# Which engine makes the low halves of the weight units between the third branch's projection and the output projection

## The reference

```python
def hybrid_layer(x, ...):
    h = rms_norm(x, norm1_g)
    z = h @ w_in
    ya, yb, yc, yd = retention(..), conformer_conv(..), spatial_gating(..), swa_attention(..)
    ys = jnp.stack([ya, yb, yc, yd], axis=2)
    branches = jnp.einsum('bsnc,ncd->bsnd', ys, w_branch)   # four projections, 512 -> 1024
    mix = jnp.sum(sigmoid(zg) * branches, axis=2)
    x = x + (mix @ w_out)                                   # 1024 -> 1024
    h = rms_norm(x, norm2_g)
    gt, up = jnp.split(h @ w_ffn_in, 2, axis=-1)
    return x + ((silu(gt) * up) @ w_ffn_out)
```

## Time and profile before

| | |
|---|---|
| median of 3 runs | 2315.18 us (2309.21 to 2315.8) |
| profiled execution, its own time | 2315.32 us |
| its span | 2313.9 us |
| TensorE's granted clock, mean | 0.988 of full speed |
| PE busy | 2202.0 us (95%) |
| PEld busy | 2047.3 us (88%) |
| DVE busy | 1401.4 us (61%) |
| ACT busy | 1195.0 us (52%) |
| POOL busy | 869.1 us (38%) |
| transfers | 369.58 MB, mean 160 GB/s |

### The profile page before, as it was taken

The page is one execution under the profiler, slowest core; times in us unless marked ns, Lnnn a source line. Parts: engine busy times, 40 slices in busy tenths (PEclk is TensorE's granted clock), DMA queues, the critical chain, the costliest instruction groups (busy, mean ns, idle before and its releaser), DMA issues.

```text
span 2313.9 us, 38008 instructions
## 1 busy us (share of the span) xinstructions
PE 2202.0 (95%) x15186; PEld 2047.3 (88%) x15186; DVE 1401.4 (61%) x2409; ACT 1195.0 (52%) x2050; POOL 869.1 (38%) x477
## 2 busy tenths in 40 slices
PE   8888889999999979999999999999999999899999
PEld 7888879999999867888888799898998889899997
DVE  5758761586844597666665764446664665546664
ACT  6546434554444696554555355555444355555443
POOL 5555366687600392000003666460000766461000
PEclk9999999999999999999999999999999999999999
DMA  6443355555565404666665545355565554345555
GB/s 224 137 123 108 118 158 170 173 165 177 178 184 183 136 1 127 191 194 194 194 192 183 173 146 159 109 159 166 183 184 176 155 155 158 115 148 166 182 184 161
DMA packets 102930, 369.58 MB, mean 160 GB/s; under 512 B 11362, under 2 KB 13794, under 8 KB 102116
## 3 DMA queue, kind: packets, MB, share of 16 engines
q1 hardware_dynamic: 102756, 367.15, 51.4%
HBM read 364.49 MB, written 2.62 MB: 159 GB/s over the span
## 4 chain that ended last, share of the span: by engine, by line
PE 74%; DVE 17%; ACT 6%; issue 2%; DMA 1%; POOL 1%; SPq 0%; DVEq 0%; ACTq 0%
PE stream_bank L530 13%; PE stream_bank L531 13%; PE stream_bank L532 13%; PE side_bank L530 10%; PE side_bank L532 10%; PE side_bank L531 10%; DVE first_hot L1961 2%; DVE experts L1951 2%; ACT unit_hi L1046 1%; PE side_bank L592 1%; DVE unit_lo L1556 1%; POOL unit_lo L2284 1%; ACT squares L1072 1%; PE side_bank L611 1%; DVE hot L1919 1%
## 5 line engine op out<-in xcount | busy, mean ns | idle before, releaser
L2284 POOL TENSOR_TENSOR unit_lo<-raw,unit_hi 128x1024 fp32r<-128x1024 f32 (+1 forms) x305 | 744.6, 2447 | 445.1 <-ACT unit_hi L1046 444.6
L1046 ACT ACTIVATE unit_hi<-raw 128x1024 fp32r<-128x1024 f32 (+1 forms) x678 | 708.0, 1045 | 188.3 <-PE side_bank L532 92.9
L1556 DVE TENSOR_TENSOR unit_lo<-raw,unit_hi 128x1024 fp32r<-128x1024 f32 x373 | 459.4, 1232 | 403.4 <-ACT unit_hi L1046 403.0
L530 PE MATMUL stream_bank<-hT_hi,unit_hi 128*128 128x256 f32 x1672 | 494.0, 295 | 3.5 <-DVE unit_lo L1556 3.5
L531 PE MATMUL stream_bank<-hT_lo,unit_hi 128*128 128x256 f32 x1672 | 477.8, 286 | 0.0
L532 PE MATMUL stream_bank<-hT_hi,unit_lo 128*128 128x256 f32 x1672 | 477.6, 286 | 0.0
L530 PEld LDWEIGHTS stream_bank<-hT_hi,unit_hi 128*128 128x128 f32 x1672 | 325.7, 195 | 12.3 <-issue 6.3
L530 PE MATMUL stream_bank<-h2T_hi,unit_hi 128*128 128x256 f32 x1152 | 327.4, 284 | 2.6 <-DVE unit_lo L1556 2.5
L531 PEld LDWEIGHTS stream_bank<-hT_lo,unit_hi 128*128 128x128 f32 x1672 | 325.8, 195 | 1.6
L531 PE MATMUL stream_bank<-h2T_lo,unit_hi 128*128 128x256 f32 x1152 | 326.7, 284 | 0.0
L532 PE MATMUL stream_bank<-h2T_hi,unit_lo 128*128 128x256 f32 x1152 | 326.6, 284 | 0.0
(11 more groups left out here) (341 smaller groups left out, 4099.2 us busy)
## 6 DMA issues: line engine op xcount, KB each, us to landing
raw<-in_peer_u_dram SPq DMA_DIRECT2D x128, 512.0 KB, 3.6
raw<-in_peer_v_dram SPq DMA_DIRECT2D x128, 512.0 KB, 4.2
raw<-in_gate_dram SPq DMA_DIRECT2D x64, 512.0 KB, 3.6
raw<-in_gt_dram SPq DMA_DIRECT2D x44, 512.0 KB, 3.6
raw<-in_up_dram SPq DMA_DIRECT2D x44, 512.0 KB, 3.7
raw<-in_ffn_out_dram SPq DMA_DIRECT2D x44, 512.0 KB, 4.0
raw<-in_branch_dram SPq DMA_DIRECT2D x32, 512.0 KB, 3.7
raw<-in_w_gate_dram SPq DMA_DIRECT2D x24, 512.0 KB, 3.6
```

Source lines behind the costliest of these rows:

```text
L530: mm(out, l.hi, r.hi, start=start, stop=False)
L1046: activation(k.unit_hi[n % SPLIT_SLOTS][:, 0:w], k.raw[n % RAW_SLOTS][:, 0:w], ACT.Copy).then_inc(k.sem("unit_hi"), 1)
L1556: V.tensor_tensor(k.unit_lo[s][:, 0:w], k.raw[n % RAW_SLOTS][:, 0:w], k.unit_hi[s][:, 0:w], ALU.subtract).then_inc(unit_lo, 1)
L2284: G.tensor_tensor(k.unit_lo[s][:, 0:w], k.raw[n % RAW_SLOTS][:, 0:w], k.unit_hi[s][:, 0:w], ALU.subtract).then_inc(k.sem("unit_lo_pool"), 1)
```

## The change

One bound of a range in `lo_count` is moved, once for each of the two hybrid layers. The range in which DVE makes every low half began eight units before the first feed-forward unit (the first `w_out` unit), plus AHEAD, so at unit 19. Now it begins at the first unit of the third branch projection, plus AHEAD, so at unit 11. Unit 12 divides by 8 and is DVE's already. So seven units for each layer (11 and 13 to 18), fourteen in all, go from POOL to DVE. Nothing else is changed: TensorE's, ACT's and SP's instructions keep their order, and wait for the same units' low halves on the other engine's semaphore.

```diff
@@ -265,7 +265,7 @@
 
         U = self.place_of
         alone = [(U["peer_u", LATE // 1024] + AHEAD, U["cg.0", 0] + AHEAD)]
-        alone += [(U[f"gt.{l}", 0] - 8 + AHEAD, U[f"ffn_out.{l}", KF - 1] + 1 + AHEAD) for l in range(LAYERS)]
+        alone += [(U[f"branch.{l}", BRANCH_ORDER[2] * KD // 2] + AHEAD, U[f"ffn_out.{l}", KF - 1] + 1 + AHEAD) for l in range(LAYERS)]
         self.lo_engine, self.lo_ready = [], []
         counts = {"dve": 0, "pool": 0}
         for n in range(len(self.plan)):
```

## The result

The median went from 2314.61 us (2309.21 to 2318.37, 14 runs) to 2319.53 us (2317.83 to 2323.31, 14 runs). The ratio is 1.0023, with a 95% interval of 1.0016 to 1.0031: slower by 3.7 to 7.2 us, 4.9 by the medians. That is within the 0.3% that I called "the same", and yet not nothing. The profiled execution took 2318.88 us, of which the span is the first line here.

What follows compares the result with a forecast made beforehand. TensorE was taken to bound the kernel, never waiting for POOL. Two layers at 1.6 us, 3.2 us in all, on a profiled 2315.32 us or a median of 2315.18 us gave 2318.4 us, range 2311 to 2325.

Steps and rivals of the forecast that it cites:

- Third projection, cost nothing: Low halves 11, 13, 14: each 1.23 us fits DVE's idle 1.46 us per unit, so no cost and no gain.
- The loop of 4.23 us: Fourth projection: DVE and ACT wait on each other, so each unit takes 4.23 us against TensorE's 2.88.
- Low half 19 late, PE idle 0.6 us: At `w_out`: low half 19 ends 0.5 us too late for TensorE, which idles 0.6 us.
- High half 22, low half 23, high half 26: Behind low half 19, loads and adds slip; high half 26 waits for its load until 1583.24, not 1581.62.
- 1.6 us a layer, 3.2 in both: Late high half 26 delays the second norm by 1.6 us per hybrid layer, containing PE's 0.6 us; bounds +1.0 and +3.8.
- The ports: DVE's splits no longer share SBUF ports with POOL: two holdups, 0.7 us a layer, freed without shortening the sum.
- The clock behind the turns stays at 1.00: After the second norm's turns in the hybrid layers, TensorE's granted clock was to stay 1.00, adding no cost.
- Rival 2: Long landings delay the norm and TensorE's clock falls behind the turns: 5.9 us a layer, 2327 us; chance 0.14.
- hide part of the 1.9 us: First hybrid layer: a longer wait could hide part of the 1.9 us of issue behind the turns; given no value.

Runs made afterwards that it cites:

- e1: Kernel before with only the third projection's low halves (11, 13, 14) moved to DVE; 2315.19 us, ratio 1.0004 to before.
- e4: Changed kernel, but in the fourth projection DVE makes the low half between the sum and its split, not ahead of the product; 2313.63 us, ratio 0.9996 to before.
- e5: Changed kernel with unit 26's high half moved behind the norm's squares on ACT, its low half behind the diagonal on DVE; 2314.57 us, ratio 1.0005 to before.
- e2: Kernel before with only the fourth projection's low halves (15 to 18) moved to DVE; 2319.13 us, ratio 1.0019 to before.
- e3: Changed kernel with 10 instead of 8 spare matmuls ahead of the second norm's turns in each hybrid layer; 2318.57 us, ratio 1.0015 to before.
- e9: Changed kernel with the hybrid layers' spare matmuls replaced by 21 on split operands with 512 columns; 2318.96 us, ratio 1.0024 to before.
- e7: Kernel before with two useless ACT copies ahead of the second norm's squares in each hybrid layer, no low half moved; 2318.91 us, ratio 1.0019 to before.
- e11: Kernel before with 11 instead of 8 spare matmuls ahead of the second norm's turns in the hybrid layers; 2316.26 us, ratio 1.0016 to before.
- e8: Changed kernel measured and profiled again without any edit; 2318.53 us, ratio 1.0020 to before.
- e10: Changed kernel with the orders of e4 and e5, 7 spare matmuls in the hybrid layers, first block as it was; 2312.91 us, ratio 0.9998 to before.
- e6: Changed kernel with the edits of e4 and e5, 16 spare matmuls in the first block, 7 in the hybrid layers; 2314.10 us, ratio 0.9999 to before.

## Why the prediction was right, and where not

The time came at 2319.53 us, with 2318.4 predicted and 2311 to 2325 as the range. The change was to cost 3.2 us and cost 4.9 us; part of that gap of 1.7 us is hidden in the time, since the forecast started from a median before of 2315.18 us, which later runs put at 2314.61 us. By its steps:

- **Third projection, cost nothing.** Right, shown by e1.
- **The loop of 4.23 us.** Right: 4.21 us. e4 shows that it was the loop and not the sum of DVE's work, which is 3.06 us.
- **Low half 19 late, PE idle 0.6 us.** It came 1569.80 - 1561.35 = 8.45 us behind the first `w_out` matmul (8.64 predicted), and PE reached the spare matmuls 22.25 - 21.79 = 0.46 us late. The view of waits shows only 0.2 us of it for L1556: the wait of 0.16 us in the row of 1569.86 is the gap that the trace sees, and the rest shows in no row of its own. For so short a loss the distance between two landmarks is the better measure.
- **High half 22, low half 23, high half 26.** 12.12, 15.55 and 20.72 us behind the first `w_out` matmul, where 12.46, 15.89 and 20.94 were predicted. Each is earlier by the 0.2 us of low half 19 and a little more, as the loads landed in 3.6 and 3.9 us. High half 26 was released by its transfer, as forecast, and e5 shows that this is what carries the loss to the norm.
- **1.6 us a layer, 3.2 in both.** 1.40 and 1.30 us, 2.7 in both. Mis-sized by 0.5 us, for the reason above. In e2 the second layer lost 2.1 us, so the size also hangs on the landings.
- **The ports.** DVE's splits all take 0.69 us in the fourth projection, where one took 1.07 beside POOL. That gain does not show in the norm distance: e4, which has it and no loop, is the kernel before in every distance.
- **The clock behind the turns stays at 1.00.** Wrong, and this is the term that was mis-sized: nothing was put down, and the middle distance grew by 1.73 us, 1.47 of them by the fall. Rival 2 had the right place with a wrong trigger. I tied the fall to the length of the wait ahead of the turns, somewhere between 1.9 and 4.3 us, and priced it at 2.1 us in each layer. It came with waits of 1.19 and 1.06 us, and with 0.18 us (e3) and none (e9), and only in the first layer. Nor could a longer wait hide part of the 1.9 us, as the prediction held possible: they are a wait for DVE's work on the same turns, and were 1.9 us in every profile.

So the median is nearer to the forecast (1.1 us) than its working deserves: 0.5 us too much in the norms, 1.7 us too little in the middle distance, 0.6 us too much in the starting time, and the runs' own spread.

**What sets the fall.** In all thirteen profiles PE has a pause of 1.9 us of issue behind the first layer's turns, at the same place in the program; the second layer has none there, and the clock never fell behind its turns. The fall came in six profiles, all with a norm distance of 26.84 us or more in the first layer, and in none of the seven with 26.55 or less. Measured to the matmul that ends the pause, it is 1594.10 - 1561.35 = 32.75 us in after, 32.53 in e7, 32.62 in e2 and e3, 32.71 in e9, all with the fall; 32.17 in e11, 31.35 in before, 31.33 in e5, all without. So the fall goes with the pause coming late, whatever made it late: the low halves (after, e2, e8), with the wait filled (e3, e9) or not, or more ACT work alone (e7). That it is the pause, and not something else behind the turns, is argued from the second layer alone; no run removed the pause.

The traces' record of the clock shows what the pause is late against. In the kernel after (columns as in the windows above):

```profile
1472.58:1595.46 122.88, 119.64 (x853) 110.69 (x852) 68.13 (x124) 68.01 (x137) 35.76 (x15) 1.00 0.48 147
1595.46:1598.87 3.41, 3.41 (x18) 3.41 (x17) 0.00 (x0) 0.37 (x2) 0.00 (x0) 0.50 0.52 154
```

In all six profiles the fall begins 122.88 us behind the clock's last rise, while it comes 1.0 to 1.4 us behind the end of the pause. Marked in the other seven, the same moment lies 1.8 us (e11) to 3.0 us (e10) behind the end of the pause. So in these profiles the fall keeps its distance to the clock's earlier step and not to the pause. That the fall comes only where the pause ends this close ahead of the moment would explain why a few tenths of a microsecond decide; it fits all thirteen profiles but is argued, and no run tests it alone.

The Trainium skill ("TensorE: Matmul & The Clock Gate", "HAM oscillation — how this bites in real kernels") warns of repeated idle stretches, with waits of 3 to 5 us in its example. The traces agree that an idle stretch precedes each of these six falls, but it is one of 1.9 us and not repeated, and here the measurement decides. They show beyond it that filling the longest avoidable wait (e3, e9) did not help.

**What the pause is.** The view of waits calls it issue, but the trace has PE's sequencer standing at a semaphore. First and second layer of the kernel after (durations in ns, first start), and DVE's last operations of the norm in the first:

```profile
L548 PEldq EVENT_SEMAPHORE  x1: 2687/2687/2687, 1591.4 to 1591.4; - x1
L548 PEldq EVENT_SEMAPHORE  x1: 51/51/51, 2127.1 to 2127.1; - x1
1590.44 3.56 DVE L1586 SCALAR_TENSOR_TENSOR hT_lo<-side_bank,cols,hT_hi 128x256 fp32r<-128x256 f32 x8 [2.18 <-ACT hT_hi L1082]
```

DVE's last split of the turned X ends at 1590.44 + 3.56 = 1594.00 us and PE's next matmul starts at 1594.10; in all thirteen profiles it is 0.10 us. The banks of PSUM, the memory that matmuls write to, go round for the feed-forward units (L543). In the first layer the first of them gets the side bank of the last turns, which is free only when DVE has split it, and the semaphore that PE's sequencer waits for is the one that this split raises. In the second layer it gets a stream bank and starts right behind the turns. So the pause belongs to the norm and moves with it, and another bank for this one unit should remove it; no run did that.

## What to carry to other kernels

Before giving an idle engine more work, find its place in the queue, not its share of busy time: a step that waits for another engine's result, which itself waits for this engine, makes a loop, and the loop's length replaces the sum of the work (4.21 us for 2.88 here; the same step one place later cost nothing). Follow a late result through the buffers it frees and the loads behind them to the next step that someone waits for, and see whether another order takes that step out from behind the load, as e5 does with the norm and unit 26. Ask of a pause that the profile calls issue which semaphore the sequencer stands at, since here it was a bank still in use. When a late stretch is followed by a pause of TensorE, price both levels of the clock: here 0.3 us more of lateness (26.84 against 26.55 us) brought another 1.5 us.

## What the runs showed of the hardware

- A delay of 1.2 to 1.4 us (norm distance) ahead of an unchanged pause of 1.9 us turned a granted clock of 1.00 into 0.50 for some 3.4 us, in every profile of the kernels that had it (six) and in none of the others (seven). It costs 1.5 us up to the next norm's turns (198.2 us behind the first turns with it, 196.6 to 196.7 without).
- The pause itself, called issue by the view, was TensorE's wait for a PSUM bank: its next matmul started 0.10 us behind DVE's last reading of that bank in all thirteen profiles.
- Spare matmuls without any idle time ahead of the turns did not hold the clock up (e9, 0.51 in the window behind). In the first block the clock stayed up in the one profile with more of them: with the wait at 0.77 us in place of 4.27, the window had 1.00 (e6), while it fell there in the twelve others.
- A fall of the clock had a fixed distance to the step before: 122.88 us behind the last rise in all six profiles that have it.
- ACT's table load (1.28 us) and half of the norm's squares fit ahead of the adds if no transfer stands before them: 0.84 us of norm distance in each layer (e6, e10 against e4).
